# One core's hybrid decoder step: the delta state read by keys, gate tiles emptied bank by bank, and three gate tiles moved to the memory attention

## The reference

```python
proj = h @ w_in + b_in            # dn_qkv, dn_z, dn_b, dn_a, lru_x, lru_g, fq, fk, fv, ff, fg, mq, mg, gate (4 x 1024)
# A: gated delta rule, in chunks; S: state, g: cumulated log decay
u = u0 - w @ S ;  [u0, w] = solve(I + strict(beta * decay * k k^T), [beta * v, beta * exp(g) * k])
o = exp(g) * q @ S + (decay * q k^T) @ u ;  S = exp(g_end) * S + kdec^T @ u
# B: RG-LRU;  C: forgetting attention ("fox"), causal, logits + c[t] - c[s];  M: attention to 256 memory tokens
up = [branch_n @ w_branch_n for n in 4] ;  merged = sum(sigmoid(gate_n) * up_n) ;  y = x + merged @ w_out
```

## Time and profile before

| | |
|---|---|
| median of 3 runs | 1699.66 us (1695.4 to 1700.04) |
| the profiled execution | 1700.4 us |
| its span, first to last instruction | 1698.7 us |
| mean granted TensorE clock | 0.996 |

### The profile page before, as it was taken

How to read it: one execution, slowest core, us unless ns; L and a number is a source line. 1 busy time by engine, 2 the same in 40 slices (tenths; PEclk the granted TensorE clock), 3 DMA queues, 4 the chain that set the end, 5 groups by cost and what they waited for, 6 DMA issues and landing times. The chain is left out here.

```text
span 1698.7 us, 26352 instructions
## 1 busy us (share of the span) xinstructions
PE 1636.0 (96%) x10771; PEld 1563.4 (92%) x10771; DVE 844.9 (50%) x1240; ACT 535.5 (32%) x898; POOL 519.2 (31%) x387
## 2 busy tenths in 40 slices
PE   5999999999999999999999999999999999989999
PEld 4989998999999999999889899999989999889976
DVE  4656753244433331771176763435668451985611
ACT  6322342222222222133244433321145222654300
POOL 1434415433433411821244551222211211103400
PEclk9999999999999999999999999999999999999999
DMA  4212144222221112633266352235210332434521
GB/s 154 52 25 53 49 134 132 69 69 69 70 69 57 38 50 83 184 101 99 81 193 194 107 175 100 69 114 156 68 37 26 106 95 75 143 112 140 153 82 57
DMA packets 189365, 163.19 MB, mean 96 GB/s; under 512 B 18380, under 2 KB 157055, under 8 KB 188726
## 3 DMA queue, kind: packets, MB, share of 16 engines
q1 hardware_dynamic: 189246, 161.51, 32.5%
HBM read 131.38 MB, written 30.22 MB: 95 GB/s over the span
## 5 line engine op out<-in xcount | busy, mean ns | idle before, releaser
L276 POOL TENSOR_TENSOR wL<-w_raw,wH 128x1024 fp32r<-128x1024 f32 (+1 forms) x112 | 242.7, 2167 | 805.4 <-ACT wH L269 805.4
L316 PE MATMUL ps<-hH,wH 128*128 128x344 f32 x1920 | 447.4, 340 | 18.0 <-ACT d_gate L1814 4.6
L316 PE MATMUL ps<-hL,wH 128*128 128x344 f32 x1920 | 410.1, 320 | 0.0
L316 PE MATMUL ps<-hH,wL 128*128 128x344 f32 x1920 | 408.5, 320 | 0.0
L316 PEld LDWEIGHTS ps<-hH,wH 128*128 128x128 f32 x1920 | 311.7, 190 | 31.3 <-issue 18.1
L316 PEld LDWEIGHTS ps<-hL,wH 128*128 128x128 f32 x1920 | 324.4, 189 | 0.0
L316 PEld LDWEIGHTS ps<-hH,wL 128*128 128x128 f32 x1920 | 321.9, 188 | 0.0
L269 ACT ACTIVATE wH<-w_raw 128x1024 fp32r<-128x1024 f32 (+1 forms) x116 | 108.5, 935 | 113.8 <-PE ps L316 107.3
L2870 POOL TENSOR_SCALAR fa_logits<-fox_c_bc,token_scalars 128x128 f32<-128x128 f32 (+7 forms) x32 | 61.6, 1925 | 58.1 <-DMA fox_c_bc<-rows_g_c_beta 30.2
L1830 ACT ACTIVATE d_m<-ps 128x512 f32<-128x512 f32 x48 | 28.6, 595 | 142.2 <-PE ps L2006 142.2
L316 PE MATMUL ps<-branch_in_r,wH 128*128 128x344 f32 x288 | 61.1, 320 | 0.0
(11 more groups left out here) (574 smaller groups left out, 2816.2 us busy)
## 6 DMA issues: line engine op xcount, KB each, us to landing
w_raw<-in_w_in SPq DMA_DIRECT2D x80, 512.0 KB, 5.1
m_th<-gate_spill SPq DMA_DIRECT2D x28, 516.0 KB, 4.2
gate_spill<-d_gate SPq DMA_DIRECT2D x18, 516.0 KB, 3.0
fa_kv<-in_cache_fox_k SPq DMA_DIRECT2D x32, 256.0 KB, 3.0
fa_kv<-in_cache_fox_v SPq DMA_DIRECT2D x32, 256.0 KB, 3.5
w_raw<-in_w_branch SPq DMA_DIRECT2D x32, 256.0 KB, 2.8
gate_spill<-fa_gate SPq DMA_DIRECT2D x10, 516.0 KB
x_rows<-in_x_prompt SPq DMA_DIRECT2D x8, 512.0 KB, 7.1
```

Source lines behind the costliest of these rows:

```text
L276: pool.tensor_tensor(self.wL[:, t % 2, 0:nk], self.raw_at(t)[:, 0:nk], self.wH[:, t % 2, 0:nk].bitcast(F32), ALU.subtract).then_inc(self.w ...
L316: last = pe.matmul(self.ps[:, b + g, 0:cols], w[:, t % 2, k], x[:, k, g * cols:(g + 1) * cols], start=(k == 0 and n == 0), stop=(k == nk - ...
```

## The change

- The delta state is read by keys: slot 10 multiplies the keys with the state (`of_keys`, into bank 4), VectorE scales the result by beta and decay and subtracts it from VB (`rest`), and slot 13 makes one product of Y and that. `solved`, KBG, and ScalarE's negated copy go.
- Gate tiles get a kind of their own ("gate"): ScalarE empties the first bank alone, then the other two (`evac_by_bank`); the next tile's first step starts when the first bank is empty and takes its nine matmuls bank by bank.
- `FirstChunk.late_act` acts at tile 5 in place of 3.
- In both attentions the first two scores go ahead of TensorE's wait for all that the stage before leaves.
- The decode queries are broadcast into two buffers in turn, QB and DLG.
- Three gate tiles of merge 3 go from the fox to the memory attention, behind the four of `mg` (`SiluAndGates`): 7 tiles in each.

```diff
 
         kind = self.tiles[t][2]
         n = sum(1 for x in self.tiles[:t + 1] if x[2] == kind)
+        if kind == "gate":
+            return self.evac_gate, 2 * n
         return (self.evac_act if kind == "act" else self.evac_dve), n
+
+    def evac_by_bank(self, act, t, dst):
+
+        n, d = self.gate_of[t]
+        b, r = self.tiles[t][3], BROW["gate"] + KD * n + d
+        bias = self.hbias[:, r:r + 1]
+        act.activation(dst[:, 0:G3], self.ps[:, b, 0:G3], ACT.Tanh, scale=0.5, bias=bias).then_inc(self.evac_gate, 1)
+        act.activation(dst[:, G3:TOK].rearrange("p (a b) -> p a b", a=2), self.ps[:, b + 1:b + 3, 0:G3], ACT.Tanh,
+                       scale=0.5, bias=bias).then_inc(self.evac_gate, 1)
 
     def project_step(self, pe, t, xH, xL, k, groups=3, cols=G3, only=None):
 
         _, nk, _, b = self.tiles[t]
         only = range(groups) if only is None else only
+        by_bank = False
         if k == 0 and 0 in only:
             pe.wait_ge(self.w_lo, t + 1)
             before = [u for u in range(t) if self.tiles[u][3] == b]
+            by_bank = bool(before) and self.tiles[before[-1]][2] == "gate"
             if before:
-                pe.wait_ge(*self.emptied(before[-1]))
-        for n, (w, x) in enumerate(((self.wH, xH), (self.wH, xL), (self.wL, xH))):
-            for g in only:
-                last = pe.matmul(self.ps[:, b + g, 0:cols], w[:, t % 2, k], x[:, k, g * cols:(g + 1) * cols],
-                                 start=(k == 0 and n == 0), stop=(k == nk - 1 and n == 2))
+                sem, count = self.emptied(before[-1])
+                pe.wait_ge(sem, count - 1 if by_bank else count)
+        passes = list(enumerate(((self.wH, xH), (self.wH, xL), (self.wL, xH))))
+        order = [(n, w, x, g) for n, (w, x) in passes for g in only]
+        if by_bank:
+            order = [(n, w, x, g) for g in only for n, (w, x) in passes]
+        for at, (n, w, x, g) in enumerate(order):
+            if by_bank and at == len(passes):
+                pe.wait_ge(sem, count)
+            last = pe.matmul(self.ps[:, b + g, 0:cols], w[:, t % 2, k], x[:, k, g * cols:(g + 1) * cols],
+                             start=(k == 0 and n == 0), stop=(k == nk - 1 and n == 2))
         if k == nk - 1 and groups - 1 in only:
...
 
             def late_act(self, act, j):
-                if j == 3:
+                if j == 5:
                     act.wait_ge(S["diff"], 1)
                     act.activation(DT[:], DT[:], ACT.Exp).then_inc(S["decay"], 1)
...
                     pool.wait_ge(S["kn"], ch + 1)
                     pool.wait_ge(S["sc"], 3)
-                    g.step(pool.tensor_tensor(KBG[:, ch % 2], KN[:], bc(SC[:, 0, ch]), ALU.mult))
                     pool.tensor_tensor(KD_[:, ch % 2], KN[:], bc(SC[:, 1, ch]), ALU.mult).then_inc(S["kb"], 1)
...
                         if s == 9 and ch + 1 < NCH:
                             prepare_rows(ch + 1)
-                        if s == 12:
-                            act.wait_ge(S["wT"], ch + 1)
-                            act.activation(M1[:], BM, ACT.Identity, scale=-1.0).then_inc(S["wTe"], 1)
...
                     dve.tensor_copy(Y[:], BY).then_inc(S["upy"], 1)
 
+                def rest(ch):
+                    dve.wait_ge(S["ks"], ch + 1)
+                    dve.tensor_tensor(KS[:, ch % 2], BX, bc(SC[:, 0, ch]), ALU.mult).then_inc(S["rest"], 1)
+                    dve.wait_ge(S["rest"], 2 * ch + 1)
+                    dve.wait_ge(S["vb"], ch + 1)
+                    dve.tensor_tensor(VB[:, ch % 2], VB[:, ch % 2], KS[:, ch % 2], ALU.subtract).then_inc(S["rest"], 1)
...
                     level(ch, 5)
                     decayed(ch)
                     turned_x(ch, 6)
+                    rest(ch)
                     level(ch, 6)
                     state(ch)
...
                     pe.wait_ge(S["nu"], ch + 1)
                     if ch:
-                        pe.wait_ge(S["wTe"], ch)
+                        pe.wait_ge(S["m1e"], ch * LV)
                     for h in range(H):
...
                         last = pe.transpose(B[7][:, h], O[:, h], K.ident[:])
                     last.then_inc(S["oT"], 1)
 
-                def solved(ch):
-                    pe.wait_ge(S["upy"], (ch + 1) * (LV + 1))
-                    pe.wait_ge(S["kb"], ch + 1)
-                    for h in range(H):
-                        last = pe.matmul(BM[:, h], KBG[:, ch % 2, h], Y[:, h], start=True, stop=True)
-                    last.then_inc(S["wT"], 1)
-
-                def values(ch):
-                    pe.wait_ge(S["wTe"], ch + 1)
+                def of_keys(ch):
+                    pe.wait_ge(S["upx"], (ch + 1) * LV)
                     if ch:
                         pe.wait_ge(S["state"], ch)
                     else:
                         pe.wait_ge(S["zero"], 1)
                     for h in range(H):
-                        pe.matmul(BX[:, h], Y[:, h], VB[:, ch % 2, h], start=True, stop=False)
-                        last = pe.matmul(BX[:, h], M1[:, h], ST[:, h], start=False, stop=True)
+                        last = pe.matmul(BX[:, h], kT(ch, h), ST[:, h], start=True, stop=True)
+                    last.then_inc(S["ks"], 1)
+
+                def values(ch):
+                    pe.wait_ge(S["upy"], (ch + 1) * (LV + 1))
+                    pe.wait_ge(S["rest"], 2 * ch + 2)
+                    for h in range(H):
+                        last = pe.matmul(BX[:, h], Y[:, h], VB[:, ch % 2, h], start=True, stop=True)
                     last.then_inc(S["u"], 1)
...
                 def added(ch):
                     pe.wait_ge(S["ue"], ch + 1)
+                    pe.wait_ge(S["kb"], ch + 1)
                     for h in range(H):
...
                             rows(ch + 1)
-                        if s == 12:
-                            solved(ch)
+                        if s == 10:
+                            of_keys(ch)
                         if s == 13:
...
 
-def attend(K, KT, V, RQ, Q, tag, fox, t0, nt, new_bulk, branch=None):
+class SiluAndGates:
+
+
+    def __init__(self, silu, gates):
+        self.parts, self.silu = (silu, gates), silu.silu
+
+    def part(self, t):
+        return self.parts[1 if t >= self.parts[1].t0 else 0]
+
+    def act(self, act, t): self.part(t).act(act, t)
+
+    def dve(self, dve, t): self.part(t).dve(dve, t)
+
+    def sync(self, sp, t): self.part(t).sync(sp, t)
+
+    def left(self, eng):
+        for x in self.parts:
+            x.left(eng)
+
+
+def attend(K, KT, V, RQ, Q, tag, fox, t0, nt, new_bulk, turned, branch=None):
 
...
 
                 def load_q(b):
 
-                    if b:
-                        sp.wait_ge(M["used"], b)
-                    sp.dma_start(QB[:], K.d_q[b:b + 1].rearrange("b h d -> b (h d)").broadcast_to([P, H * P])
-                                 ).then_inc(M["qb"], 16)
+                    if b >= 2:
+                        sp.wait_ge(M["used"], b - 1)
+                    sp.dma_start(ROWS2[b % 2][:], K.d_q[b:b + 1].rearrange("b h d -> b (h d)").broadcast_to([P, H * P])
+                                 ).then_inc(M[f"qb{b % 2}"], 16)
 
...
                 sp.dma_start(K.d_q, QR).then_inc(M["q_out"], 16)
                 sp.wait_ge(M["q_out"], 16)
                 load_q(0)
+                load_q(1)
                 if fox:
                     sp.dma_start(Q3[:], K.d_q.rearrange("b h d -> (b h) d")).then_inc(M["row_in"], 16)
...
                     K.project_step(pe, t, K.hH, K.hL, k)
                     if 1 <= x <= NORMS:
                         last_norms(pe, x - 1, NORMS)
+                pe.wait_ge(*turned)
+                pe.wait_ge(*K.emptied(t0 - 2))
+                pe.wait_ge(*K.emptied(t0 - 1))
+                scores(0)
+                scores(1)
                 before(pe)
                 for h in range(H):
                     last = pe.transpose(BANK[0:NB, h * P:(h + 1) * P], Q(h, slice(SEQ, TOK)), K.ident[:])
                 last.then_inc(M["q"], 1)
-                scores(0)
-                scores(1)
                 for n in range(len(its)):
...
 
                     dve.wait_ge(M[f"k_in{b % 2}"], per_load * (b // 2 + 1))
-                    dve.wait_ge(M["qb"], 16 * (b + 1))
+                    dve.wait_ge(M[f"qb{b % 2}"], 16 * (b // 2 + 1))
                     kv = KV[:, b % 2]
                     flat = kv.rearrange("p g h d -> p g (h d)")
-                    dve.tensor_tensor(flat, flat, QB[:].unsqueeze(1).broadcast_to([P, NP, H * P]), ALU.mult
+                    dve.tensor_tensor(flat, flat, ROWS2[b % 2][:].unsqueeze(1).broadcast_to([P, NP, H * P]), ALU.mult
                                       ).then_inc(M["used"], 1)
...
         at = {}
         here = [[], [0, 1], [0], [0]]
         apart = [(n, d) for d in range(KD) for n in range(4) if d not in here[n]]
-        with_delta, with_fox = apart[0:18], apart[18:28]
+        with_memory = [(3, d) for d in range(KD - 3, KD)]
```

(14 more changed lines are left out.)

36 lines of the change are left out of this document (17 added, 19 removed).

## The result

The changed kernel takes 1693.01 us (median of 9 runs, 1688.17 to 1694.27), the kernel before 1700.04 (9 runs on the same chip): a ratio of 0.9958 with a 95% interval of 0.9942 to 0.9973. That is 7 us, 0.42%, faster, and the interval leaves out 1. The prediction said 1674, 1663 to 1684, so the direction was right and the size was not. The profiled execution took 1691.95 us with a span of 1690.3.

The account below looks back on a forecast made before the run. TensorE's own work was taken to set the time nearly everywhere, except in the memory attention, where it waits for VectorE. Delta −11.2, first chunk −5, fox −33.5 and memory +24 made −25.7 off 1699.7: 1674 us, range 1663 to 1684.

Parts of the forecast that it names:

- Delta by keys: Delta stage: reading the state by keys saves 6.8 us of products and 0.7 of work changes; VectorE's added operations cost nothing.
- Gates by bank: Gate tiles emptied bank by bank cut TensorE's waits: −3.7 us in delta, about −1.7 in fox; bounds 0 and −7.2.
- First chunk: Delta rule's beginning: first chunk's exponentials at tile 5 instead of 3 save 5.0 us; bounds −1 and −6.2.
- Scores early: Both attentions: first two scores ahead of TensorE's wait save about 1.0 us in each, 0 to 1.6.
- Memory: Memory attention: takes three gate tiles, partly into TensorE's idle time, 107 to 131 us, +24; bounds +21 and +32.
- Fox: Fox attention: gives up three gate tiles, −38 less 4.5 of new stalls, 214 to 180.5 us, −33.5; bounds −38 and −20.
- E: Rival, chance 0.03: fox paced by its chain from POOL difference back to POOL, stays at 214 us; whole slower, 1707 us.
- B: Rival, chance 0.15: fox turns VectorE/POOL-bound, keeps 8 to 14 us of what it should lose; 1682 to 1688 us.
- A: Main case, chance 0.60: the terms come as summed over all stages, 1668 to 1680 us.
- C: Rival, chance 0.18: memory +21, fox −38 and not held, delta with all waits; about 1666, 1661 to 1668 us.
- D: Rival, chance 0.04: B, and memory fills nothing (+32); about 1695 us, no measurable change.
- The last spill: Merge 3's start: waiting for the third gate's way to memory costs nothing; bound +3 us if the spill is slow.

Follow-up runs that it names:

- e11: e1 with the delta state read as before (KBG, its eviction, eight products a chunk), gates still evicted by bank: 1682.6 us, ratio 0.9904.
- e10: The changed kernel with the delta rule's gate tiles emptied in one piece as before: 1699.0 us, ratio 0.9996.
- e12: e1 with two old starts: first scores behind the decode queries in both attentions, first chunk's exponentials at tile 3: 1683.3 us, ratio 0.9903.
- e1: The changed kernel with the three moved gate tiles back in the fox attention: 1677.4 us, ratio 0.9875.
- e2: The changed kernel with the next head's row c loaded ahead of the decode loads of its step in SyncE's order: 1688.5 us, ratio 0.9941.
- e3: The changed kernel with POOL's low part of the next weights one query tile later in its order: 1682.1 us, ratio 0.9905.
- e5: The changed kernel with both fox reorders, those of e2 and e3, together; seven tiles in fox: 1678.4 us, ratio 0.9873.
- e7: e5 without most of VectorE's multiplication of the decode keys in the fox attention (one column kept): 1674.0 us, ratio 0.9852.
- e9: The changed kernel with both fox reorders and one gate tile in place of three moved to the memory attention: 1671.5 us, ratio 0.9835.
- e4: The changed kernel without most of VectorE's multiplication of the decode keys in the fox attention (one column kept): 1686.9 us, ratio 0.9935.
- e14: The changed kernel with one gate tile in place of three moved to the memory attention, without the two reorders: 1681.1 us, ratio 0.9901.

## Why the prediction was right or wrong

Each name is a term of the prediction's sum, with what it said in brackets.

**Delta by keys** (−6.8 − 0.7): right, 7.3 by e11. `rest` was free, as the count of 2 us of cover said: with it TensorE is idle for 0.4 of 345 us.

**Gates by bank** (−3.7 in the delta rule): too small, 6.6 by e10. Its bound did not hold it either: all the waits for the delta's gates are 4.6 us, and the 7.2 that I named contain fox's 2.6. I counted the waits that the view names. Each of them has more behind it: the small waits for `d_x` (1.5 us) went with them, and 2.3 us of the 352 are in TensorE's busy column and not in its idle time (346.9 busy against 344.6). The sign that I had named, no wait above 0.2 us, was missed by one wait of 0.7. In fox (−1.7) the waits fell from 2.6 us to 0.3, but the span shows nothing of it: e12, which has ten tiles, gates by bank and the scores where they were, has 312.7 us, and the kernel before 312.3.

**First chunk** (−5): the number is right, 5.3, but only in part by its reason, which is luck. The exponentials' place, from which I had the whole term, is 3.1 of it by e12; the other 2.2 are not from KBG (e11 has it back and the same 277.6), and stay open.

**Scores early** (−1 each, at most 1.6): 3.0 in fox, 0 in memory.

**Memory** (+24): right, +23.1, as the sum of parts that I had otherwise. By the windows TensorE's busy time rose by 30.5 us where the forecast has 33.1 (34.1 + 2.2 less 3.2 of clock), and its idle time fell by 6.5 where the forecast has 9.0: two misses of about 2.5 us that cancel, which is luck. The three tiles cost 27.6, and 4.5 us were saved without them (204.2 to 199.7). Since the scores' place is nothing there (e12), what is left in the change is the second row of decode queries: VectorE's waits for `ma_qb` (4.3 us in three places before) are gone. No run took that buffer alone away, so this is argued by exclusion and not shown.

**Fox** (−33.5): the step that failed. With the ten tiles left in fox, the rest of the change gave 2.6 us (312.3 to 309.7, e1) where 2.7 were forecast, so what failed is the move's own part. Of the forecast's −38 before stalls 12.9 us came (312.3 to 299.4). The failing step is the price of the stalls that appear when the filler goes: +4.5, for VectorE's runs of decode steps alone, and of POOL's differences and the row of c only the sentence that they are "now hidden behind TensorE and would show more", at no price. The runs put about 25 us in that place (38 less 12.9). Of these the c row in SyncE's order is 5.3 (e2), POOL's low part in front of the differences 9.5 (e3), both together 15.2 (e5), and VectorE's key products 4.0 more (e7). The rest of 6 us was not taken apart. The bound of −20 did not hold −12.9, and the reason given for it does not lead to it: with half of VectorE's 72 us of idle time left, the stage would be 178 us, which is −36. The signal that I had named, waits of TensorE for fox logits of over 10 us, was itself too coarse: that wait is 9.7 us, and 6.4 stand under another name.

Both waits could be read in the earlier trace rows as 30 us each; I took them to be hidden for good because TensorE was idle for only 6.7 us. That idle time said how much was uncovered, not how much was covered.

**Rivals.** E named the true mechanism, the chain POOL, VectorE, ScalarE, TensorE, which the tiles had only filled, and I gave it 0.03 because TensorE was idle for only 6.7 us. It decides from 25.7 us of stalls beyond the sum's; 20.6 came (12.9 measured, 33.5 forecast), so the change stayed on the faster side. B had the place, and with the fixed order and the c row, which it names as reasons, a part of the cause, but not the size (8 to 14), and neither engine is the bound: VectorE has 57 of 201 us to spare and POOL 107, and what held them was mostly order. The longer POOL operations which I weighed for B came as well, but as some 6 us and not the 95 weighed there, and in e5 POOL is back to 89.8 us; how much of fox's time hangs on them, no run shows. A and C, which both need fox to give up 33 to 38 us, fell with that row; D fell with memory's +23.1.

**The last spill** (0): right. In the kernel after, the first branch tile's products start at 1540.40, right behind the gate tile's last at 1539.93, without idle time, and the last thing that VectorE waited for in front of them was the attention's own last output:

```profile
1535.24 1.33 DVE L1123 TENSOR_TENSOR branch_in<-b_m_gate,branch_in 128x24 f32<-128x24 f32 x2 [13.14 <-ACT branch_in L3201]
...
1539.93 0.63 PE L335 MATMUL ps<-hH,wL 128*128 128x344 f32 x3
1540.40 0.32 PE L335 MATMUL ps<-b_m_gate_r,wH 128*128 128x344 f32 x1
```

**Was the move worth it?** Not for three tiles; for one, with the reorders, it was. By tile, with both reorders, fox gives 11.1, 6.9 and 8.4 us (310.6, 299.5, 292.6, 284.2), and memory takes 4.3, 11.9 and 11.4 (199.7, 204.0, 215.9, 227.3). The first tile falls into memory's 8 us of idle time (95.14 busy of the first 103 us in e1), the others find none:

```profile
1417.00:1520.00 103.00, 95.14 (x643) 88.95 (x642) 86.33 (x171) 59.52 (x178) 8.10 (x3) 0.98 0.40 116
```

Against the runs of the kernel before beside them, the kernel after without its move (e1) is 21 us faster, and with one tile moved and both reorders (e9) 28 us.

## What to carry to other kernels

Before independent work is taken out of a stage, list the waits that it covers, by the waits of the engines off the path as well as by TensorE's idle time, and look in each queue for what stands ahead of the late instruction without needing to: here two changes of order gave back 15 of the 25 us that had been covered. Price moved work at the margin and not by its mean: the first tile cost its new stage 4 us and the next two 12 each. And a stage that is full hides mistakes of order: the same two edits were worth 15 us with seven tiles, about 10 with nine, and nothing that can be told from zero with ten.

## What the runs showed of the hardware

With 18 us of VectorE's products left out (e4), POOL did the same work of the stage in 85.0 us in place of 93.8, in nearly the same stretch:

```profile
824.00:1016.00 192.00, 175.39 (x1136) 154.47 (x1135) 125.55 (x197) 80.06 (x201) 84.96 (x64) 0.99 0.50 144
```

In e7, against e5, it is 5.2 us of POOL for 15.8 of VectorE (142.4 to 126.7). So a third to a half of a microsecond of POOL's time hangs on each microsecond of such VectorE work; that is my estimate from these two pairs. It goes the other way too: the same VectorE operations of two SBUF inputs (groups of instructions, e9 first, then e14, without the two reorders) took 13.0 and 15.3 us, and 9.1 and 11.7:

```profile
L3132 DVE TENSOR_TENSOR fa_kv<-fa_kv 128x1024 f32<-128x1024 f32 x8 | 13.0, 1630 | 0.3
...
L3082 DVE TENSOR_TENSOR fa_kv<-fa_kv,fa_d_logits 128x2048 f32<-128x2048 f32 x4 | 9.1, 2278 | 4.4 <-DMA fa_kv<-in_cache_fox_k 4.4
```
```profile
L3132 DVE TENSOR_TENSOR fa_kv<-fa_kv 128x1024 f32<-128x1024 f32 x8 | 15.3, 1911 | 0.3
L3082 DVE TENSOR_TENSOR fa_kv<-fa_kv,fa_d_logits 128x2048 f32<-128x2048 f32 x4 | 11.7, 2930 | 0.0
```

VectorE's reductions of the same keys, with one input, took 18.3 us in both:

```profile
L3085 DVE TENSOR_REDUCE fa_scores<-fa_kv 128x16 f32<-128x2048 f32 x8 | 18.3, 2286 | 0.3
```

The Trainium skill (GPSIMD Engine Reference, "Specifications") says that GpSimd shares its SBUF interfaces with VectorE and contends with VectorE's operations of two SBUF inputs. By that rule, the trace agrees.

A wait can cost more than the view of waits says: with 3.9 us fewer of them (4.6 in nine places to 0.7 in one) the delta rule was 6.6 us shorter (e10).
